# First attention of a two-layer trunk: the output product between the next step's first two row minima, and a weight exchange spread over other key tiles

## The reference, cut to what matters

```
logits = einsum('bthd,btkd->bhtk', qb, ks) * HEAD_DIM ** -0.5     # qb: 128 queries of a head
logits = logits + bias[rel_bucket(sel - tpos)]                    # unselected keys: -inf
p = softmax(logits)
b_out = einsum('bhtk,btkd->bthd', p, vs)                          # 16 heads x 64
mix = concatenate([a_out, b_out]) @ w_out                         # w_out: 2048 x 1024
```

## Time and profile before

| what | value |
|---|---|
| runs | 2518.41, 2519.82, 2527.75 us, median 2519.82 |
| profiled execution, its own time | 2515.06 us |
| its span, first to last instruction | 2512.8 us |
| PE busy | 2407.7 us, 96% of the span |
| mean granted TensorE clock | 0.986 |
| first attention | about 465 to 797 us after the start |
| output products L2348 | 32, of 0.68 to 0.69 us |

### The profile page before, as it was taken

One profiled execution on the slowest core, in us unless ns is written; L12 is line 12 of the kernel. 1 busy time (PEld: TensorE's weight loads), 2 busy tenths in 40 slices (PEclk: granted clock), 3 DMA queues, 4 the chain that ended last, 5 costly groups with the idle time before them and its releaser, 6 DMA issues.

```text
span 2512.8 us, 34098 instructions
## 1 busy us (share of the span) xinstructions
PE 2407.7 (96%) x11680; PEld 1985.4 (79%) x11680; DVE 1700.9 (68%) x2859; ACT 1182.8 (47%) x2025; POOL 1471.1 (59%) x813
## 2 busy tenths in 40 slices
PE   7899999998998999999999999989999999999997
PEld 6689888776876878888778887878777888778886
DVE  5469999676775596555656677167787565666676
ACT  5442633566664374444333336165665444433331
POOL 2111578655553149877678642456637888577951
PEclk9999999999999999999999999989999999999999
DMA  5390544833645624554644444756553545754343
GB/s 148 67 133 26 127 105 138 252 102 92 177 122 168 230 70 144 166 153 151 238 168 157 144 134 135 173 135 175 143 191 101 157 140 166 246 184 150 102 143 133
DMA packets 330515, 369.63 MB, mean 147 GB/s; under 512 B 14002, under 2 KB 229586, under 8 KB 328324
## 3 DMA queue, kind: packets, MB, share of 16 engines
q1 hardware_dynamic: 321748, 351.96, 48.0%
q10 hardware_dynamic: 8352, 15.21, 2.0%
q0 software_dynamic: 272, 0.62, 0.1%
HBM read 237.18 MB, written 130.55 MB: 146 GB/s over the span
## 4 chain that ended last, share of the span: by engine, by line
PE 66%; DVE 6%; ACT 4%; issue 3%; DMA 2%; SPq 0%; POOL 0%; DVEq 0%; ACTq 0%; POOLq 0%
PE ps L468 62%; PE ps L2757 2%; PE ps L2836 1%; DMA h_operand_raw<-h_operand_scratch 1%; ACT logits L1706 1%; PE ps L2766 1%; DVE logits L2273 1%; DVE acc L1957 1%; DVE probs_T L2308 1%; ACT probs_T L1731 1%; ACT junk L1389 1%; DVE acc L1976 0%; PE ps L2846 0%; DVE xn_T L2060 0%; ACT xn_T L1425 0%
## 5 line engine op out<-in xcount | busy, mean ns | idle before, releaser
L468 PE MATMUL ps<-xn_T,w_split 128*128 128x512 f32 (+1 forms) x2928 | 677.5, 390 | 2.2 <-ACT x_sums L1433 2.0
L468 PEld LDWEIGHTS ps<-xn_T,w_split 128*128 128x128 f32 (+1 forms) x2928 | 547.2, 187 | 120.1 <-DVE xn_T L2060 2.5
L468 PE MATMUL ps<-w_operand,h_operand 128*128 128x512 f32 x2016 | 463.6, 392 | 13.4 <-DVE acc L2542 6.7
L468 PEld LDWEIGHTS ps<-w_operand,h_operand 128*128 128x128 f32 x2016 | 381.1, 189 | 95.8 <-issue 13.0
L423 POOL TENSOR_TENSOR w_split<-w_raw,w_split 128x1024 fp32r<-128x1024 f32 x74 | 189.0, 2564 | 448.4 <-ACT w_split L416 448.1
L1303 POOL TENSOR_TENSOR w_split<-w_raw,w_split 128x512 fp32r<-128x512 f32 x168 | 244.3, 1467 | 102.0 <-ACT w_split L1821 100.6
L468 PE MATMUL ps<-x_sums_high,w_split 128*128 128x512 f32 x896 | 284.9, 389 | 0.0
L2544 DVE TENSOR_TENSOR acc<-acc,ps 128x512 f32<-128x512 f32 x288 | 185.8, 680 | 130.4 <-PE ps L468 129.9
L1335 POOL TENSOR_TENSOR w_operand<-w_block,w_operand 128x2048 fp32r<-128x2048 f32 x42 | 207.3, 4937 | 109.7 <-ACT w_operand L1841 109.7
L1828 ACT ACTIVATE h_operand<-h_operand_raw 128x2048 fp32r<-128x2048 f32 (+1 forms) x56 | 95.3, 1702 | 262.8 <-DMA h_operand_raw<-h_operand_scratch 262.8
L2474 DVE TENSOR_TENSOR h_operand<-h_operand_raw,h_operand 128x2048 fp32r<-128x2048 f32 (+1 forms) x56 | 164.8, 2944 | 56.6 <-ACT h_operand L1828 56.5
(11 more groups left out here) (284 smaller groups left out, 4256.5 us busy)
## 6 DMA issues: line engine op xcount, KB each, us to landing
h_operand_raw<-h_operand_scratch SPq DMA_DIRECT2D x42, 1024.0 KB, 5.1
w_raw<-in_w SPq DMA_DIRECT2D x72, 512.0 KB, 8.1
w_block<-in_w SPq DMA_DIRECT2D x48, 512.0 KB, 6.1
q_scratch<-q_split SPq DMA_DIRECT2D x128, 128.0 KB, 2.6
cat_scratch<-attn_out_split SPq DMA_DIRECT2D x128, 128.0 KB, 2.6
w_raw<-in_w_in SPq DMA_DIRECT2D x30, 512.0 KB, 5.1
q_tile<-q_scratch ACTq DMA_DIRECT2D x58, 256.0 KB, 2.7
unit_tile<-cat_scratch SPq DMA_DIRECT2D x56, 256.0 KB, 4.1
```

The costliest lines, as they stand in the source:

```text
L468: return nc.tensor.matmul(out_ap, stat, mov, start=start, stop=stop)
```

## The change

Four edits. DVE's output product of step g is issued in step g + 1, after the minima of head 0 of step g + 2 and before those of head 1. The exchange of weights is moved: high parts of tiles 4 to 7 at the end of (1, 4), after tile 5 of (1, 5), at the end of (1, 5), after tile 5 of (1, 6); low parts of 4 and 5 ahead of the output in (1, 5), of 6 behind it, of 7 ahead of the output in (1, 6). Tiles 8 and 9: high parts after tiles 5 and 6 of (3, 6), low parts ahead in (3, 7); tiles 10 and 11: high parts at the end of (3, 7), low parts behind its output. The step without a fill in head group 3 is (3, 0) instead of (3, 6), so fills 26 to 31 are each one step later. Fill 16 in (1, 6) and fill 31 in (3, 6) get plans of their own.

```
-            n = 2 if (i, b) == (1, 4) else 0 if (i, b) in ((1, 5), (3, 6), (3, 7)) else 1
+            n = 2 if (i, b) == (1, 4) else 0 if (i, b) in ((1, 5), (3, 0), (3, 7)) else 1

-SWAP_STEP = {1: 5, 3: 6}
+SWAP_HIGH = {(1, 4, "end"): [4], (1, 5, 5): [5], (1, 5, "end"): [6], (1, 6, 5): [7],
+             (3, 6, 5): [8], (3, 6, 6): [9], (3, 7, "end"): [10, 11]}
+SWAP_LOW = {(1, 5): ([4, 5], [6]), (1, 6): ([7], []), (3, 7): ([8, 9], [10, 11])}

 # POOL, step (i, b), after mask_bias(g + 3)
-            if i % 2 and b == SWAP_STEP[i]:
-                n = T_O0 + 4 * (i // 2 + 1) + 2
-                split_lo(pool, n)
-                split_lo(pool, n + 1)
-                pool.wait_ge(w_lo, n + 2)
+            ahead, behind = SWAP_LOW.get((i, b), ([], []))
+            for m in ahead:
+                split_lo(pool, T_O0 + m)
+            if ahead:
+                pool.wait_ge(w_lo, T_O0 + ahead[-1] + 1)
 # ... the output's three instructions ...
-            if i % 2 and b == SWAP_STEP[i] - 1:
-                (the low parts of the first two tiles)
+            for m in behind:
+                split_lo(pool, T_O0 + m)
+            if behind:
+                pool.wait_ge(w_lo, T_O0 + behind[-1] + 1)

 # ACT, after the copy of key tile st and the exponential; and at the end of the step
-                if i % 2 and b == SWAP_STEP[i] and 1 <= st <= 4:
-                    split_hi(act, T_O0 + 4 * (i // 2 + 1) + st - 1)
+                for m in SWAP_HIGH.get((i, b, st), []):
+                    split_hi(act, T_O0 + m)
+            for m in SWAP_HIGH.get((i, b, "end"), []):
+                split_hi(act, T_O0 + m)

 # DVE
+        def output(g):
+            dve.wait_ge(pv_done, X0[g + 1])
+            dve.wait_ge(d_free, g + 1)
+            if g >= 2:
+                dve.wait_ge(ol_ok, g - 1)
+            nc.vector.tensor_tensor(osb[:, g % 2, :], ps[:, 6, :], rec[:, g % 2, :], ALU.mult).then_inc(o_ok, 1)
                 j = todo.pop(0)
                 far(g + 1, j)
                 near(g + 1, j)
+                if g and j == 0:
+                    output(g - 1)
+            if g + 1 == HG * NB:
+                output(g - 1)
-            (the product at the end of the step)
+        output(HG * NB - 1)

 # PE, fill_plan
+            if k == 16:
+                return {2: (k, 0, 1), 4: (k, 1, 2), 6: (k, 2, 3), "end": (k, 3, 4)}
+            if k == 31:
+                return {0: (k, 0, 2), 2: (k, 2, 3), 4: (k, 3, 4)}
```

## The result

The changed kernel takes 2524.27 us, the kernel before 2519.10 (medians of 20 runs each). The medians lie 5.2 us apart; the ratio of the two kernels with its 95% interval is 1.0019 [1.0010, 1.0028], which is 4.8 us (2.5 to 7.1). The change is slower, by less than the 0.5% named in the prediction, so "the same" and on the slow side, as forecast (+5.1).

The account below looks back on a forecast made before the run. PE, busy 96% of the span, was taken as the bound, its waits paid in full. 4.75 - 2.3 + 5.9 + 1.5 - 1.9 - 3.05 + 0.2 = +5.1 us gave 2524.9 us, range 2515 to 2532.

Parts of the forecast that it names:

- The product's move: Throughout the attention: the later output product delays DVE's first low part by up to 0.60 us per step, +4.75 in all.
- b = 4: Five-key-tile steps: a hole under 0.15 us leaves a price of 0.45 in three steps, 1.35; (1,4) taken as 0.
- b = 3: Four steps with a hole of 0.44 us: price up to 0.16, taken as 0.10 each, 0.4 in all.
- (1,5): First exchange: high parts leave ACT's chain of copies, so the step takes 13.1 us, a gain of 2.3.
- (1,6): First exchange: PE waits twice for POOL's low parts 6 and 7; the step ends at 20.8 us, not 14.90, +5.9.
- The clock's 1.5: At (1,6): PE's two stops bring 3.4 us at half clock, costing 1.5 us, bounds 0 and 3.4.
- Rival (a): In (1,6) POOL is in time, so 5.9 and 1.5 go: -2.3, 2517.5 us; chance 0.22.
- The later fills: (3,0) loses its 12 matmuls: gain 1.9 us, bounds 1.3 and 2.6.
- b = 0, 1, 2: Short steps: DVE waits for ACT's copy ahead of the low part, so the moved product costs 0.
- The second exchange: (3,6) takes 15.2 us, gain 3.05; half clock gone, 0.55 off (3,7); projection start +0.2 through POOL's low parts.
- Rival (b): The product's move is hidden too; with POOL in time in (1,6), -7.1, 2512.8 us; chance 0.13.
- (c): PE falls to half clock in the eight steps of six and seven key tiles: 13.6 more, 2538.5 us; chance 0.06.

Follow-up runs that it names:

- first_repaired: Changed kernel with high parts 4 to 7 at step ends, low parts 4 to 7 before (1,5)'s output, fill 16's ordinary plan: 0.9994 to the kernel before.
- repaired_product_back: first_repaired with the output product back at the end of its step: 0.9966 to the kernel before.
- low7_before_mask: Changed kernel with POOL making low part 7 straight behind low part 6, ahead of step (2,1)'s masked bias: 1.0011 to the kernel before.
- product_alone: Kernel before with only the output product moved behind the minima of the next step's head 0: 1.0031 to the kernel before.
- second_alone: Kernel before with only the change's second weight exchange (tiles 8 to 11) and later fills, product at the step's end: 0.9984 to the kernel before.
- product_back: Changed kernel with the output product put back at the end of each step, weights and fills as changed: 0.9984 to the kernel before.
- product_behind_low: Changed kernel with the output product behind the step's first low part instead of head 0's minima: one profiled execution, 2520.69 us.
- best: repaired_product_back with (1,4)'s first fill taken one key tile earlier and low parts 8 and 9 one step earlier: 0.9946 to the kernel before, median 2506.65 us.

## Why the prediction held, step by step

**The product's move** was given 4.75, 4.35 of it in the eight long steps; these measure 4.03, and 4.17 with the product moved alone. The full price of 0.60 for b = 5 and 6 is exact (0.60 to 0.63 in each of the five steps, and the waits 0.48 and 0.56 grew to 1.07 and 1.16). Mis-sized: b = 4, 0.50, 0.27 and 0.15 against 0.45, and b = 3, nothing against 0.10. Rows without a bracket bounded the hole, they did not measure it. As forecast, the steps of the first exchange carry the same 0.6: first_repaired less repaired_product_back is 0.58 in (1,5) and in (1,6).

**(1,5)**: 13.1 forecast, 13.17 and 13.18 where no fall disturbs it, 14.37 in the profile of the changed kernel, with the fall at 603.4. The forecast of the mechanism held, and a fall there was not foreseen.

**(1,6)**: 20.8 and 1.5 for the clock were forecast, 22.32 measured, through both of POOL's times. The waits were to be 2.4 and 2.9 and are 2.69 and 2.03. The clock's 1.5 is right in size and not in its form: one fall of 3.4 us was forecast, the profile has 6.8. Its first half (from 627.33) slows the work ahead of PE's second stop, which POOL ends in any case, so it only shortens that stop and costs nothing. Its second half makes the way from the last piece to the last value 3.35 us long (630.92 to 634.27) where it was 1.87 in (2,6) before (700.07 to 701.94): 1.48. Rival (a), *POOL is in time*, is refuted by the two waits. low7_before_mask takes the second away and first_repaired both.

**The later fills**: 1.9 was forecast, (3,0) and (3,1) give 1.19 together, because the moved product and its minimum stand in the way of (3,0)'s low part; with the product at the end they give 1.65. The 0.5 between is the product's, which I had counted at nothing for b = 0, 1, 2. This step of the prediction failed. (The steps of b = 2 lose 0.06 to 0.09 each besides.) The other 0.25 is (3,1), which gets longer by that much. DVE in (3,0) after:

```profile
729.15 0.69 DVE L2320 TENSOR_TENSOR attn_out<-ps,rec_den 128x512 f32<-128x512 f32 x1
729.75 0.41 DVE L2291 CUSTOM_DVE_ANT_0 logits<-ps,mask_bias 128x256 f32<-128x256 f32 x1
730.18 0.66 DVE L2311 TENSOR_TENSOR probs_T<-ps,probs_T 128x512 fp32r<-128x512 f32 x1
```

The low part follows the product and the next minimum without a hole. In the earlier trace rows it waited 1.47 for ACT's copy; with the fills gone the copy comes earlier, and that hole, which I had let cover the product, is no longer there.

**The second exchange**: (3,6) 15.2 forecast, 15.30 measured, without a fall. (3,7) and the start of the projection together +0.13 against +0.2; PE's wait for POOL before the projection:

```profile
802.94 4.71 POOL L425 TENSOR_TENSOR w_split<-w_raw,w_split 128x1024 fp32r<-128x1024 f32 x2
807.90 1.39 PE L470 MATMUL ps<-w_split,hidden 128*128 128x512 f32 x5 [1.69 <-POOL w_split L425]
```

**The range's inner bounds** do not come out of the terms. The prediction says that the bounds of the likeliest sum "taken together" give 2516 to 2533; added up they give about 2509 to 2536. The forecast of 2524.9 does not use them, but the stated range of 2515 to 2532 leans on them.

**The clock** is what was missed. The attention is longer by 8.24 in the profile, 3.1 more than the sum. 1.5 of it is the fall in (1,4) and 1.2 the one in (1,5); the product in (3,0) is 0.5, and the terms that came out smaller and larger make up the rest. The stop of 2.75 us in (1,4) is in the kernel before as well. Nine of the ten profiles have it; in seven of them a fall follows (+1.3 to +1.6), in before and in repaired_product_back none. So the profile from which I forecast was a lucky one at this point. The Trainium skill ("TensorE: Matmul & The Clock Gate", Part 1) says that the gate's monitor runs freely and does not start with the kernel, so that the point of transition varies. The traces agree for this stop: it is one and the same, with a fall behind it or without. It should have been priced as a chance in both kernels.

The same holds for (1,5) and (1,6). In product_alone and second_alone, whose weights are exchanged in these steps as before, a fall of 6.8 us lies across them; in the kernel before there is none. The fall in the changed kernel's (1,5) is missing in low7_before_mask, product_back and product_behind_low, where ACT makes the high parts in the same places.

That the medians differ by 5.2 and not by 8.2 fits with this. An estimate from the few profiles: (1,4)'s fall (1.4) comes in seven of nine, the old exchange's (about 1.6) in two of three, the new (1,5)'s (1.2) in one of four. The kernel before would then lose about 2.2 us on average that its profile does not show, the changed kernel about 1.3 less than its profile shows, and the two attentions would lie about 5 us apart. No run shows how often the falls really come, so +5.1 against 4.8 is in part luck: falls of this size were left out on both sides, and they nearly cancel.

By its ratio product_alone costs 7.8, with an interval from 5.0 to 10.6, and only about 5.8 in steps (4.17, 0.6 in each of (1,5) and (1,6), 0.26 in (3,6) and (3,7), 0.14 elsewhere). The interval holds both. Whether the moved product makes falls likelier is open.

Rival (b) is refuted by product_alone, and (c) by every profile: no step of six or seven key tiles outside the exchanges has a fall in it.

## What to carry to other kernels

Here an instruction that lay in a hole between two deliveries of the bound engine was free, and moved past one of them it cost its full spacing (0.60 us) in each step that had no hole further on. Weights prepared on a slow engine must be placed by that engine's own queue: here 6.8 us in one step, the product's 0.6 not counted, went because one low part stood behind an output that could only be finished late, and another behind a mask bias that was not due yet, while the engine had stood idle for 4.6 us. Compare steps and not spans, and hold a clock fall for the edit's own only when several profiles with the edit show it and several without it do not: (1,4)'s fall stood in seven profiles and belonged to no edit.

## What the runs showed of the hardware

A stop of 2.75 us in PE's stream cost 1.3 to 1.6 us more in half clock behind it in seven profiles, and nothing in two. In the attention the stretches at 0.50 lasted 3.4 or 6.8 us. Taking the stop away (best) was worth 3.0 us for one DVE copy moved by one key tile. Two stops, of 2.69 and 2.03 us, with 3.0 us of work between them (625.92 to 628.88), came with one stretch of 6.8 us; so did 2.67 and 1.98 in product_back. Stops of 2.11 and 1.10 at the same place (product_behind_low) came with 3.4, and so did the single one of 2.67 in low7_before_mask. I had expected 3.4 for two.
